# A two-layer hybrid kernel: decay rows made during the MLA attention, the sliding-window heads in another order, the one-expert round in the middle

## The reference

```python
# GDN: decays of a chunk, used on both k k^T and q k^T
g = jnp.cumsum(chunk(g.astype(f32)), axis=-1)
diff = g[..., :, None] - g[..., None, :]
decay = jnp.where(causal, jnp.exp(jnp.where(causal, diff, 0.0)), 0.0)
lmat = jnp.einsum("bhnid,bhnjd->bhnij", k_beta, k) * decay
a_intra = jnp.einsum("bhnid,bhnjd->bhnij", q, k) * decay
q_dec = q * jnp.exp(g)[..., None]
...
# window attention with a sink
m = jnp.maximum(jnp.max(scores, axis=-1), sink)
p = jnp.exp(scores - m[..., None])
denom = jnp.sum(p, axis=-1) + jnp.exp(sink - m)
out = jnp.einsum('bnhgqk,bnkhd->bnqhgd', (p / denom[..., None]), vv)
...
# one expert
hid = jax.nn.silu(xb @ w_gate_e[e]) * (xb @ w_up_e[e])
return hid @ w_down_e[e]
```

## Time and profile before

| | us |
|---|---|
| median of 3 runs | 1567.12 |
| lowest, highest | 1566.44, 1567.72 |
| the profiled execution | 1567.29 |
| its span in the trace | 1565.4 |
| busy in it: PE | 1470.3 |
| busy in it: DVE | 517.4 |
| busy in it: ACT | 334.9 |
| mean granted clock of PE | 0.985 |

### The profile page before, as it was taken

How to read it: one execution, slowest core, us unless ns; L and a number is a source line. 1 busy time by engine, 2 the same in 40 slices (tenths; PEclk the granted TensorE clock), 3 DMA queues, 4 the chain that set the end, 5 groups by cost and what they waited for, 6 DMA issues and landing times.

```text
span 1565.4 us, 29279 instructions
## 1 busy us (share of the span) xinstructions
PE 1470.3 (94%) x12702; PEld 1240.0 (79%) x12702; DVE 517.4 (33%) x1264; ACT 334.9 (21%) x739; POOL 3.8 (0%) x6
## 2 busy tenths in 40 slices
PE   8999989999999999899999999997999987988888
PEld 6868879978788888787778888886777766767676
DVE  0535064221334420118762542013222331222122
ACT  1152321341100000112435531102111111111111
POOL 0000000000000000000000000000000000000000
PEclk9999999999999999999999999998999999999999
DMA  8433424224344324534234443383999999999993
GB/s 321 132 116 124 162 84 152 82 81 159 118 153 162 127 69 160 204 139 162 87 109 142 148 162 123 146 341 120 418 424 423 424 423 424 424 424 424 425 424 137
DMA packets 58333, 347.37 MB, mean 222 GB/s; under 512 B 12416, under 2 KB 13536, under 8 KB 18656
## 3 DMA queue, kind: packets, MB, share of 16 engines
q1 hardware_dynamic: 55536, 339.20, 55.8%
q10 hardware_dynamic: 2672, 6.33, 1.2%
HBM read 413.21 MB, written 1.49 MB: 265 GB/s over the span
## 4 chain that ended last, share of the span: by engine, by line
PE 84%; DMA 7%; DVE 4%; issue 3%; ACT 1%; SPq 0%; DVEq 0%; ACTq 0%
PE bank L380 35%; PE bank L1018 9%; PE bank L431 8%; PE bank L394 6%; DMA work<-w_gate_e_dram 5%; PE bank L1038 5%; PE bank L1049 4%; PE bank L1062 3%; PE bank L447 2%; DVE work L1653 2%; DMA ring<-w_gate_e_dram 2%; PE bank L536 1%; PE bank L492 1%; PE bank L897 1%; PE bank L356 1%
## 5 line engine op out<-in xcount | busy, mean ns | idle before, releaser
L380 PE MATMUL bank<-hT,ring 128*128 128x256 f32 x2080 | 461.0, 382 | 3.4 <-DVE hT L1653 3.4
L380 PEld LDWEIGHTS bank<-hT,ring 128*128 128x128 f32 x2080 | 396.3, 192 | 64.3 <-issue 10.8
L1662 DVE TENSOR_TENSOR xT<-xT,bank 128x512 f32<-128x512 f32 x100 | 68.8, 688 | 330.7 <-PE bank L1038 217.4
L380 PE MATMUL bank<-work,ring 128*128 128x256 f32 x640 | 139.5, 379 | 0.0
L380 PEld LDWEIGHTS bank<-work,ring 128*128 128x128 f32 x640 | 121.3, 190 | 17.2 <-issue 1.0
L431 PE MATMUL bank<-work,ring 128*128 128x256 f32 x608 | 131.6, 379 | 0.0
L431 PEld LDWEIGHTS bank<-work,ring 128*128 128x128 f32 x608 | 115.5, 190 | 15.7
L1018 PE MATMUL bank<-work 128*32 128x128 f32 x2240 | 98.8, 274 | 13.4 <-issue 11.1
L1018 PE MATMUL bank<-ring,work 128*32 128x128 f32 x1728 | 98.3, 273 | 13.5 <-issue 10.4
L1018 PEld LDWEIGHTS bank<-ring,work 128*32 128x32 f32 x1728 | 89.6, 110 | 24.2 <-issue 24.1
L1018 PEld LDWEIGHTS bank<-work 128*32 128x32 f32 x2240 | 90.3, 110 | 20.5 <-issue 20.2
(11 more groups left out here) (325 smaller groups left out, 1521.4 us busy)
## 6 DMA issues: line engine op xcount, KB each, us to landing
work<-w_gate_e_dram SPq DMA_DIRECT2D x35, 1024.0 KB, 25.4
work<-w_up_e_dram SPq DMA_DIRECT2D x35, 1024.0 KB, 23.4
work<-w_down_e_dram SPq DMA_DIRECT2D x32, 1024.0 KB, 26.0
ring<-w_down_e_dram SPq DMA_DIRECT2D x27, 1024.0 KB, 25.4
ring<-w_gate_e_dram SPq DMA_DIRECT2D x25, 1024.0 KB, 25.6
ring<-w_up_e_dram SPq DMA_DIRECT2D x25, 1024.0 KB, 24.8
ring<-w_up_dram SPq DMA_DIRECT2D x22, 1024.0 KB, 4.9
hT<-w_gate_e_dram SPq DMA_DIRECT2D x22, 1024.0 KB
```

Source lines behind the costliest of these rows:

```text
L380: m = mm(b[:, j * SEQ:(j + 1) * SEQ], w[:, k, j * P:(j + 1) * P], tile(k), start=(k == 0), stop=(k == kt - 1))
L1662: return v.tensor_tensor(dst, a, b, ALU.add)
```

## The change

Three edits at once.

1. The decay rows earlier. SP writes the rows out ahead of unit w_qkv 0, ACT fetches `gate_rows` before the MLA attention, into the place that gateT takes later, and during that attention ACT makes `eg` (head 2) and the exponentials (heads 3 and 4), in place, and DVE adds the masks (heads 2 and 3). Only the beta rows are fetched after the last MLA product. `eg` moves out of `sq`, into the place of the blocks, so the queries are multiplied by it before `inv` is cleared and `lower_ready` is set.
2. The window attention in another order. PE turns the even head before the unit and the odd head after it, so unit h/2 + 1 stands between the transposes of heads h and h + 1, and z unit 0 takes the last such place, z unit 1 the one after. DVE and ACT do `maxima` and `exps` of two heads together, behind the odd head before them. The convolution of a unit moves up by two heads. The third silu stands at head 15, and PE's wait for the silus is split into three.
3. The round with one expert is round 11 instead of 21; the experts behind it move up by two places, with the constants of their slots.

```diff
+SHORT = GROUPS // 2
+FIRST_OF = [OWN * r if r <= SHORT else OWN * r - (OWN * GROUPS - EXPERTS) for r in range(GROUPS + 1)]
...
-    return range(OWN * r, min(OWN * r + OWN, EXPERTS))
+    return range(FIRST_OF[r], FIRST_OF[r + 1])
...
-        decay1 = area(15872, 4, 512)
+        decay1 = area(6144, 4, 512)
-        gate_rows, beta_rows = AT, TTr
+        gate_rows, beta_rows = area(6144, PROB, P), TTr
-        eg = sq[:, 0:1024].rearrange("p (h i) -> p h i", h=HEADS)
+        eg = area(24064, HEADS, P)
...
@@ PE, attention @@
-                    fill(h)
+                    if whole or h == 0:
+                        fill(h)
                     turned(h)
+                    if not whole and h % 2 == 0:
+                        fill(h + 2)
...
             def fill_xbc(h):
-                if h % 2 == 0:
+                if h < A_HEADS:
                     to_features(("xbc", h // 2), "w_xbc2", hT)
+                else:
+                    to_tokens(("z", 0), "w_z2", hT)
...
-                      lambda: to_tokens(("z", 0), "w_z2", hT))
-            to_tokens(("z", 1), "w_z2", hT)
+                      lambda: to_tokens(("z", 1), "w_z2", hT))
...
-            pe.wait_ge(S("xbc_ready"), nth("xbc_ready", 3))
+            pe.wait_ge(S("xbc_ready"), 1)
             chunk_products(0)
-            for j in range(4):
-                turn_xs(0, j)
+            pe.wait_ge(S("xbc_ready"), 2)
+            turn_xs(0, 0)
+            turn_xs(0, 1)
+            pe.wait_ge(S("xbc_ready"), 3)
+            turn_xs(0, 2)
+            turn_xs(0, 3)
@@ SP @@
-                if u == UNITS.index(("w_gates", 8, 2048)):
+                if u == UNITS.index(("w_qkv", 0, 2048)):
...
-                    if u % OWN == (SLOTS + OWN - 1) % OWN:
+                    if before_e == own_experts(before_r)[-1]:
                         overflow(KINDS.index(before_name), before_r + 1)
@@ ACT @@
-                    if h + 2 < heads:
+                    if whole and h + 2 < heads:
                         exps(h + 2)
                     fill(h)
+                    if not whole and h % 2 == 1:
+                        for g in (h + 1, h + 2):
+                            if g < heads:
+                                exps(g)
                     turned(h)
...
+            act.wait_ge(S("rows_out"), 16)
+            nc.scalar.dma_start(all_of(gate_rows), to_all(rows_dram[0])).then_inc(S("gate_rows_landed"), 16)
             def fill_mla(h):
...
+                if h == 2:
+                    act.wait_ge(S("gate_rows_landed"), 16)
+                    A_(eg[:, :, :], gate_rows[:, HEADS:PROB, :], ACT.Exp).then_inc(S("q_decays"), 1)
+                if h in (3, 4):
+                    act.wait_ge(S("grow_masked"), h - 2)
+                    for pr in range((h - 3) * HEADS, (h - 2) * HEADS):
+                        d = gate_rows[:, pr, :]
+                        m = A_(d, d, ACT.Exp, bias=ngc[:, pr:pr + 1])
+                    m.then_inc(S("decays"), 1)
...
+                if h == A_HEADS - 1:
+                    silu_xbc(8)
             attention("swa", A_HEADS, swa_out, True, sc2, PT2, fill_xbc)
-            silu_xbc(8)
@@ DVE @@
-                    if h + 2 < heads:
+                    if not sink and h + 2 < heads:
                         maxima(h + 2)
                     weights(h)
                     fill(h)
+                    if sink and h % 2 == 1:
+                        for g in (h + 1, h + 2):
+                            if g < heads:
+                                maxima(g)
...
+                if h in (2, 3):
+                    half = slice((h - 2) * HEADS, (h - 1) * HEADS)
+                    dve.wait_ge(S("gate_rows_landed"), 16)
+                    dve.wait_ge(S("q_decays"), 1)
+                    add(gate_rows[:, half, :], gate_rows[:, half, :], rep(con("neg_late"), HEADS, P))\
+                        .then_inc(S("grow_masked"), 1)
...
-            dve.wait_ge(product_ready, made("mla_o", HEADS - 1))
-            dve.wait_ge(S("gate_rows_landed"), 16)
-            mask_decays(0)
             for q in range(4):
-                dve.wait_ge(S("decays"), nth("decays"))
+                if q == 0:
+                    dve.wait_ge(S("decays"), 2)
...
+                    mul(qkvT[:, 0:HEADS, P:SEQ], qkvT[:, 0:HEADS, P:SEQ], eg[:, :, :]).then_inc(S("q_decayed"), 1)
+                    dve.wait_ge(S("q_decayed"), 1)
                     v.memset(inv[:, :, :], 0.0).then_inc(S("lower_ready"), 1)
                 conv_qkv(8 + q)
-                if q + 1 < 4:
-                    mask_decays(q + 1)
-            dve.wait_ge(S("q_decays"), 2)
-            mul(qkvT[:, 0:HEADS, P:SEQ], qkvT[:, 0:HEADS, P:SEQ], eg[:, :, :]).then_inc(S("q_decayed"), 1)
...
             def fill_xbc(h):
-                if h % 2 == 0 and h >= 2:
-                    conv_xbc(h // 2 - 1)
+                if h % 2 == 0:
+                    conv_xbc(h // 2)
```

More of the change, by code:

```diff
@@ L299, in expert_weights @@
                 return over_slots[KINDS.index(name)]
-            return expert_slots[UNIT_OF[name, min(OWN * r + j, EXPERTS - 1)] % SLOTS]
+            return expert_slots[UNIT_OF[name, min(FIRST_OF[r] + j, FIRST_OF[r + 1] - 1)] % SLOTS]
         expert_landed = [S(f"expert_weights_landed{n}") for n in range(SLOTS)]
@@ L1337, in gate_kept @@
                    at("gates", i)[:, :], ACT.Copy).then_inc(bank_free("gates", i), 1)
+            all_of = lambda a: a[:, :, :].rearrange("p h i -> p (h i)")
+            act.wait_ge(S("rows_out"), 16)
+            nc.scalar.dma_start(all_of(gate_rows), to_all(rows_dram[0])).then_inc(S("gate_rows_landed"), 16)
             def fill_mla(h):
@@ L1356, in _ @@
             act.wait_ge(product_ready, made("mla_o", HEADS - 1))
-            act.wait_ge(S("rows_out"), 16)
-            all_of = lambda a: a[:, :, :].rearrange("p h i -> p (h i)")
-            nc.scalar.dma_start(all_of(gate_rows), to_all(rows_dram[0])).then_inc(S("gate_rows_landed"), 16)
             nc.scalar.dma_start(all_of(beta_rows), to_all(rows_dram[1])).then_inc(S("beta_rows_landed"), 16)
-            for q in range(4):
-                act.wait_ge(S("grow_masked"), nth("grow_masked"))
-                if q >= 2:
-                    A_(eg[:, (q - 2) * 4:(q - 1) * 4, :], gate_rows[:, q * 4:q * 4 + 4, :], ACT.Exp)\
-                        .then_inc(S("q_decays"), 1)
-                for p in range(4):
-                    d = decay1[:, q, p * P:(p + 1) * P]
-                    m = A_(d, d, ACT.Exp, bias=ngc[:, q * 4 + p:q * 4 + p + 1])
-                m.then_inc(S("decays"), 1)
             silu_and_sine()
@@ L2328, in constants @@
     put("eps", EPS)
-    e = np.arange(EXPERTS)
     put("fold", i[:, None] % 32 == np.arange(32)[None, :])
-    put("own_base", ((e // OWN) * P + (e % OWN) * CAP)[None, :])
+    put("own_base", np.array([r * P + j * CAP for r in range(GROUPS) for j in range(len(own_experts(r)))])[None, :])
     return out
```

14 lines of the change are left out of this document (5 added, 9 removed).

## The result

| | before | after |
|---|---|---|
| median, us | 1567.42 (1566.44 to 1568.04, 4 runs) | 1540.99 (1539.59 to 1545.67, 4 runs) |
| ratio | | 0.9837, 95% interval 0.9815 to 0.9859 |
| profiled execution, us (span) | 1567.29 (1565.4) | 1540.34 (1538.3) |
| PE busy, mean granted clock | 94%, 0.985 | 95%, 0.990 |

The kernel became 26.4 us faster; 24.8 were forecast.

What follows compares the result with a forecast made beforehand. Up to the experts PE's stops set the time, among them the stream of weights. Gains of 6.5 + 7.5 + 10.8 = 24.8 us from 1567.3 gave 1542.5 us, range 1539.5 to 1550.

Steps and rivals of the forecast that it cites:

- The likeliest case: Whole kernel: all three edits gain as forecast, 1540 to 1545 us; chance 0.67.
- the prediction's own signs: Among them: PE waits under 1.5 us before line 638's products; rounds 11 to 14 take PE 19 to 20 us each.
- Edit 1, the wait: Before line 638's products, behind the MLA attention: 0.9 us of PE's 4.56 us wait is left, gain 3.6.
- the beta rows' transfer: After the last MLA product: asked for at 187.17, the beta rows take 6.41 us and land at 193.6.
- Edit 1, the clock: Behind the wait before line 638's products: the lost clock, 2.9 us, comes back, as 0.9 is nearest to harmless 0.82 us gaps.
- rival (b): At line 638, behind the MLA attention: the clock falls in spite of the short gap, 1545.4 us; chance 0.08.
- Edit 1, the cover: MLA attention: new work, 1.3 of DVE's 5.4 us free and 2.6 of ACT's 13.2, costs PE nothing.
- Edit 2: Sliding-window attention: all gaps close, giving 5.9 us of PE waits and 1.6 of clock, 7.5 us.
- The 1.3 us in hand on DVE: Sliding-window attention: DVE has the next even head's weights after some 8.4 us, PE wants them after 9.7.
- Edit 3: Experts: later loads come 15.0 us sooner and decide the end; last down products at 1542.2 instead of 1553.04, gain 10.8 us.
- Rival (e): Experts: after round 11 the loads run dry, a unit costs 4.9 us instead of 2.5, slower than before; chance 0.02.

## Why the prediction was right, and where it was off

The forecast was 1542.5 us in 1539.5 to 1550; the median is 1540.99. The likeliest case is the one that happened, at each of its three places. That the sum fits so well is luck in part. The places of the edits gave 24.65 us where 24.8 were forecast, but with errors of -0.8, +2.1 and -1.45 that cancel, and the further 1.8 that the medians show are within the interval (22 to 29 us less) and near to what the profiled execution won where no edit works. Of the prediction's own signs two weren't met: the wait is 1.70 us and not under 1.5, and three of the rounds 11 to 14 take 20.3 to 21.0 us, not 19 to 20. The sizes:

**Edit 1, the wait**: 0.9 us forecast, 1.70 measured. The mis-sized term is the beta rows' transfer. I gave it the 6.41 us of the earlier trace rows; it took 7.16 (asked for at 186.31, landed at 193.47). The work behind it takes 4.90 us, where 4.85 were forecast.

**Edit 1, the clock**: forecast to come back because 0.9 us is near to the gaps of 0.82. The gap was 1.70, as long as the one of the earlier trace rows that had a fall behind it, and there was no fall. The result was right, the reason wasn't: by my own rule this would have been rival (b), 1545.4. A gap's length alone doesn't tell: here the clock is at 1.00 behind 1.70 us, and before it is at 0.51 behind 1.67 us. PE's timeline and the stretch at that place of before:

```profile
739.89 0.55 PE L545 MATMUL bank<-con_sb,work 128*128 128x128 f32 x3 [1.67 <-DVE work L1666]
```
```profile
740.40:743.90 3.50, 3.50 (x14) 2.49 (x14) 1.75 (x7) 0.88 (x3) 0.00 (x0) 0.51 0.38 162
```

What decides whether a fall follows a gap, no run shows.

**Edit 1, the cover**: ACT's and DVE's new work in the MLA attention costs PE nothing, as forecast: from the first product with a weight unit to the point behind that attention it is 173.98 us in both kernels.

**Edit 2**: 7.5 forecast, 9.6 in the stage and 9.5 alone. The waits (5.9) and the clock (1.6) came as forecast. The term that was missing: a pair costs PE 9.38 us of work where it was 9.64 besides the 0.82 of gap, seven times 0.26 = 1.8 us. The unit, now behind transposes and not behind scores, takes 7.07 instead of 7.17. The transposes of the two heads take 0.42 and 0.38 from start to start, where they took 0.49 (up to the gap) and 0.48. This second part is a cost of the gap and not of the order, for six transposes in a row without a gap between them took 0.83 before:

```profile
749.87 0.90 PE L545 MATMUL bank<-con_sb,work 128*128 128x128 f32 x6
```

So I had priced a gap at its idle time alone, and PE's other work as the same in another order. The 1.3 us in hand on DVE was enough: no wait of any length is left.

**Edit 3**: 10.8 forecast, 9.35 measured. The mechanism is right in each step: rounds 11 to 14 take PE 20.6, 19.1, 20.3 and 21.0 us, the rate stays at 423 to 425 GB/s, the time from issue to landing falls from 26 us at unit 109 to 16 at unit 116 (9 to 11 were forecast) and is back at 25 by unit 156, and the last round waits for its loads. The size is off since the loads ended 1.5 us later on the old scale than forecast: they lead by 17.7 us at the first unit and by 16.2 at the last. In the trace of before the landings are 2.5 us apart but for one of 3.8 every 26 units or so; after, they have more irregular ones of 3.0 to 3.3. In the run with the short round at 20 that 1.5 us isn't lost (the last landing is 437.55 us behind the first down products, 439.09 in the changed kernel), and with the short round at 11 to 18 it is (438.9 to 439.2). But the shorter line of loads is not its cause as far as is known: 0.5 of it is gone by unit 108, before the short round acts, and 0.6 more come behind unit 186. The cause stays open.

**Rival (e)** was rightly small at 11. The run with the short round at 2 shows its mechanism and its price, 8.2 us, less than the 24.8 that it would have had to eat.

## What to carry to other kernels

Where a stream of transfers sets the pace of a stage and the engine has work left when the stream is over, take a short portion of work out of the end and put it into the middle: behind the point from which the transfers lead, so that enough of them are in flight to bridge the move, and so far ahead of the end that the engine can catch up. Here the stage won 9.35 us with the short round at 11 of 0 to 21; at 2 it took 8.2 us more than that, at 20 7.7 more. Work that an in-order engine does late for a consumer is best moved by following who waits for whom between two of the consumer's steps, as in the pairs of heads; the waits at three stages of this serial kernel added up (7.3 + 9.5 + 9.5 us alone, 26.4 together), and could be costed one by one. Gains of 2 to 3 us here are below what the stops of PE and the falls of its clock move by themselves (2.7 us in the last round of one run, 3.8 us ahead of the experts in another).

## What the runs showed of the hardware

**The same gap, with and without a fall of the clock.** Line 772 waits 1.53 us for DVE in all variants of the changed kernel. With the short round at 18, whose instructions there are the same as the changed kernel's, the clock is at half behind it (first stretch); in the changed kernel it is full (second, PE alone):

```profile
339.10:342.50 3.40, 3.37 (x6) 1.56 (x7) 2.00 (x4) 2.28 (x4) 0.00 (x0) 0.50 0.00 0
```
```profile
337.00:341.00 4.00, 2.89 (x10) 1.00 0.00 0
```

With the short round at 20, two places (406.1 to 412.9 and 641.6 to 648.4) are at half for 6.8 us, where the changed kernel has none at the one and 3.4 us at the other. That is 3.8 of the 4.5 us by which its experts start later. Another 1.1 is there by the first product with a weight unit (13.20 instead of 12.12), since PE waits 0.71 us for the first work on the input, which lands later, and the profile's record of the full clock begins at 10.1 instead of 8.7; 0.4 come back in front of the experts. With the short round at 18 the start is the larger part: 1.65 of the 2.3 us are there by that first product, 0.2 come from a longer wait behind the MLA attention (1.9 us), and the fall at 339.1 costs 0.7, of which 0.25 come back. All this is unchanged code. In the nine executions of the kernel before that ran beside these three, the three longest (1569.22 to 1569.86) have the lowest mean clocks (0.982 to 0.984), the other six 0.986 to 0.988: the longest executions are those with the most time at half clock.

**Stops of PE at fixed places of its instructions.** In dense runs of expert products PE stops for up to 3.17 us at places that are fixed in its instruction stream, one in 256 instructions (101 places in 26000, 102 in 26102, and as many packets of 16 KB on the instruction queue); not every place has a stop in every execution, and a stop ends 2.2 to 2.6 us behind the start of such a packet. Behind most of the long ones (2.1 to 3.1 us in these two traces) the clock is at half for 3.4 us: before at 1255.9, 1330.9, 1412.9 and 1481.1, after at 1237.5, 1268.2 and 1449.1. Ahead of the last round of the changed kernel both cost nothing: a stop of 2.85 us ends at 1448.80, with a fall behind it, and the last down products start 0.20 us behind the last landing all the same. In the last round they do cost: in the three runs with a stop of 2.1 to 3.2 us there, those products start 1.8 to 2.7 us behind that landing.
